# Leaving the 16 meta tokens out of the query side of a hybrid mLSTM / state-space layer

## The reference, cut to what matters

```python
h_p = concatenate([meta_tokens, x_prompt])          # 16 + 256 rows
mix, new = mixer_block(rmsnorm(h), ...)             # scans run over all 272 rows
h = h + mix
if drop_meta: h = h[:, N_META:]                     # the meta rows are dropped here
h = h + hier_moe(rmsnorm(h))
...
s   = (q_t . k_s) * exp(dmat[t, s] - m[t])          # causal, all s <= t
num = s @ v + ...;  den = sum_s s + ...             # mLSTM
h_a = num / max(|den|, exp(-m)) -> rms norm -> * sigmoid(za)
y   = (c_t . b_s) * decay[t, s] * dt[s] @ x + d_skip * x -> * silu(zb) -> group rms norm
out = concatenate([h_a, y]) @ w_out
```

## Time and profile before

| | us |
|---|---|
| median of three runs | 810.22 |
| the runs | 811.71, 810.21, 810.22 |
| span of the profiled execution | 805.8 |
| TensorE / VectorE / ScalarE / GpSimd busy | 772.3 / 291.0 / 217.5 / 29.1 |
| weight loads of TensorE busy | 400.1 |

### The profile page before, as it was taken

The page is one execution under the profiler, slowest core; times in us unless marked ns, Lnnn a source line. Parts: engine busy times, 40 slices in busy tenths (PEclk is TensorE's granted clock), DMA queues, the critical chain, the costliest instruction groups (busy, mean ns, idle before and its releaser), DMA issues.

```text
span 805.8 us, 9663 instructions
## 1 busy us (share of the span) xinstructions
PE 772.3 (96%) x3789; PEld 400.1 (50%) x3789; DVE 291.0 (36%) x722; ACT 217.5 (27%) x612; POOL 29.1 (4%) x85
## 2 busy tenths in 40 slices
PE   7999999998999999999999999999999998999995
PEld 5876777776767778633333333333333333233232
DVE  4945535678988420331130031121120201302204
ACT  4237656728654100340101100101001011001013
POOL 7000000001000100000000000000000000000000
PEclk9999999999999999999999999999999999999998
DMA  9943556675886749479999999999999999999992
GB/s 249 338 165 96 194 168 204 184 260 141 249 276 196 302 155 420 181 283 429 426 427 425 429 428 425 429 425 429 427 427 426 428 425 430 426 428 427 425 403 86
DMA packets 76540, 263.69 MB, mean 327 GB/s; under 512 B 7446, under 2 KB 46618, under 8 KB 62904
## 3 DMA queue, kind: packets, MB, share of 16 engines
q1 hardware_dynamic: 74704, 259.02, 82.3%
q0 software_dynamic: 1568, 3.91, 1.4%
q10 hardware_dynamic: 216, 0.07, 0.1%
HBM read 251.15 MB, written 11.99 MB: 327 GB/s over the span
## 4 chain that ended last, share of the span: by engine, by line
PE 78%; DMA 10%; DVE 7%; ACT 2%; issue 1%; POOL 1%; DVEq 0%; POOLq 0%; ACTq 0%
PE bank L2296 23%; PE bank L2375 11%; PE bank L1869 10%; PE bank L2146 7%; DMA arena<-in_w_down 5%; DMA arena<-in_w_up 5%; PE bank L1857 4%; PE bank L2321 4%; PE bank L2255 3%; PE bank L1962 2%; DVE h_tok L1406 2%; PE bank L2309 1%; PE bank L2265 1%; PE bank L1816 1%; PE bank L2023 1%
## 5 line engine op out<-in xcount | busy, mean ns | idle before, releaser
L2296 PE MATMUL bank<-ring,arena 128*64 128x512 f32 x704 | 159.2, 596 | 5.2 <-DMA ring<-in_w_up 3.7
L1869 PE MATMUL bank<-arena,ring 128*128 128x280 f32 x448 | 113.2, 407 | 3.6 <-DVE arena L1547 1.5
L2296 PEld LDWEIGHTS bank<-ring,arena 128*64 128x64 f32 x704 | 47.9, 137 | 102.2 <-issue 91.0
L1869 PEld LDWEIGHTS bank<-arena,ring 128*128 128x128 f32 x448 | 83.7, 191 | 26.0 <-issue 4.4
L507 DVE COPY arena<-bank 64x512 f32<-64x512 f32 x15 | 10.2, 683 | 205.4 <-PE bank L2375 205.4
L2375 PE MATMUL bank<-ring,arena 128*64 128x512 f32 x304 | 68.1, 593 | 3.0 <-DMA ring<-in_w_down 3.0
L1734 DVE TENSOR_TENSOR arena<-bank,WG 128x512 f32<-128x512 f32 x16 | 16.9, 1057 | 129.8 <-PE bank L2296 129.8
L2146 PE MATMUL bank<-arena,ring 128*128 128x264 f32 x256 | 58.7, 388 | 0.0
L2296 PE MATMUL bank<-arena 128*64 128x512 f32 x240 | 55.6, 598 | 2.0 <-DMA arena<-in_w_up 1.2
L2146 PEld LDWEIGHTS bank<-arena,ring 128*128 128x128 f32 x256 | 48.1, 190 | 9.4 <-issue 1.5
L1200 ACT ACTIVATE arena<-bank 128x512 f32<-128x512 f32 x15 | 9.0, 597 | 147.8 <-PE bank L2309 147.8
(11 more groups left out here) (384 smaller groups left out, 833.9 us busy)
## 6 DMA issues: line engine op xcount, KB each, us to landing
ring<-in_w_gate SPq DMA_DIRECT2D x22, 2048.0 KB, 25.0
ring<-in_w_up SPq DMA_DIRECT2D x22, 2048.0 KB, 28.5
ring<-in_w_down SPq DMA_DIRECT2D x19, 2048.0 KB, 27.2
arena<-in_w_down SPq DMA_DIRECT2D x11, 2048.0 KB, 30.7
ring<-in_w_in SPq DMA_DIRECT2D x9, 2048.0 KB, 11.7
arena<-in_w_up SPq DMA_DIRECT2D x5, 2048.0 KB, 25.3
arena<-in_w_gate SPq DMA_DIRECT2D x5, 2048.0 KB, 30.9
out<-h_tok SPq DMA_DIRECT2D x16, 512.0 KB, 5.2
```

The costliest lines, as they stand in the source:

```text
L1869: last = mm(b[:, 0:T], slot_k(UNIT_SLOT[u], 512)[:, k, o:o + P], hT[:, k, :], start=(k == 0), stop=(k == KD - 1))
L2296: last = mm(b[CAP * half:CAP * (half + 1), :], XG[:, k, (e % 2) * CAP:(e % 2 + 1) * CAP], w(kk)[:, half * 512:(half + 1) * 512], start=(k ...
```

## The change

The query side leaves out the meta columns. Gate tiles, queries, the first of three blocks of scores, weighted sums and denominators, the squares and their sums, the heads' and groups' scales and the gate products run over columns 16 to 280 (or 272, or 304) where they ran from 0. Keys, values, the convolution, `xbc` tiles and states stay as they are, and so do all waits, the order on each engine and all transfers. The core of the diff:

```diff
+Q_FROM = [META, 128, 256]
-BLK = [0, NP, NP + NP - 128]
+BLK = [0, NP - META, NP - META + NP - 128]
...
-            nc.vector.scalar_tensor_tensor(out=YB[:, c, 0:NP], in0=CBX[:, c, 0:NP], scalar=XE[:, c, 16:17],
-                                           in1=bank[6 if c % 2 == 0 else 0][:, 0:NP], op0=ALU.mult, op1=ALU.add)\
+            nc.vector.scalar_tensor_tensor(out=YB[:, c, META:NP], in0=CBX[:, c, META:NP], scalar=XE[:, c, 16:17],
+                                           in1=bank[6 if c % 2 == 0 else 0][:, META:NP], op0=ALU.mult, op1=ALU.add)\
...
-                a.activation(qT[:, h % 2, :], bank[0][:, 0:W], ACT.Copy).then_inc(s.q_sb, 1)
+                a.activation(qT[:, h % 2, META:W], bank[0][:, META:W], ACT.Copy).then_inc(s.q_sb, 1)
...
-                a.activation(dst[:, n % KD, :], z_bank(n)[:, 0:T], ACT.Tanh, scale=0.5).then_inc(signal, 1)
+                a.activation(dst[:, n % KD, META:T], z_bank(n)[:, META:T], ACT.Tanh, scale=0.5).then_inc(signal, 1)
...
-                    w = NP - t0
-                    last = v.scalar_tensor_tensor(out=ARG[0:m, n % 2, BLK[j]:BLK[j] + w], in0=b[0:m, t0:NP],
-                                                  scalar=TM[0:m, j, key:key + 1], in1=mask[0:m, 0:w],
+                    q0 = Q_FROM[j]
+                    last = v.scalar_tensor_tensor(out=ARG[0:m, n % 2, BLK[j]:BLK[j] + NP - q0], in0=b[0:m, q0:NP],
+                                                  scalar=TM[0:m, j, key:key + 1], in1=mask[0:m, q0 - t0:NP - t0],
...
-                link(v.reciprocal(SCL[0:HA, :], SCL[0:HA, :]))
+                link(v.reciprocal(SCL[0:HA, META:T], SCL[0:HA, META:T]))
...
-            def b5_tile(u, o, use, b=bank[5]):
+            def b5_tile(u, o, use, b=bank[5], q0=0):
...
-                    last = mm(b[:, 0:T], slot_k(UNIT_SLOT[u], 512)[:, k, o:o + P], hT[:, k, :], start=(k == 0), stop=(k == KD - 1))
+                    last = mm(b[:, q0:T], slot_k(UNIT_SLOT[u], 512)[:, k, o:o + P], hT[:, k, q0:T], start=(k == 0), stop=(k == KD - 1))
...
-                b5_tile(U_Z + n // 4, (n % 4) * P, B5_Z + earlier, z_bank(n))
+                b5_tile(U_Z + n // 4, (n % 4) * P, B5_Z + earlier, z_bank(n), META)
...
-                mm(bank[0][:, 0:W], wq[:, h, :], XC[:, h, :], start=True, stop=True).then_inc(s.q_ps, 1)
+                mm(bank[0][:, META:W], wq[:, h, :], XC[:, h, META:W], start=True, stop=True).then_inc(s.q_ps, 1)
...
-                mm(bank[7][0:HA, 0:NP], strip[:, 7 - h:15 - h], SQT, start=(h == 0), stop=(h == HA - 1),
+                mm(bank[7][0:HA, META:NP], strip[:, 7 - h:15 - h], SQT, start=(h == 0), stop=(h == HA - 1),
...
-                mm(bank[3][:, 0:T], col(ident[0:HA, :], k), SCL[0:HA, :], start=True, stop=True).then_inc(s.hbc_ps, 1)
+                mm(bank[3][:, META:T], col(ident[0:HA, :], k), SCL[0:HA, META:T], start=True, stop=True).then_inc(s.hbc_ps, 1)
```

More of the change, by code:

```diff
@@ L272, in y_sq @@
         def y_sq(c):
-            return rowt(9 + c % 3, NP)
+            return rowt(9 + c % 3, NP - META)
         h_tok = sb("h_tok", [P, 3, D])
@@ L1505, in denominators @@
             def denominators():
[L1507 to L1511, removed]
+                rows = bank[7][32:32 + HA, META:T]
+                link(v.tensor_copy(DEN[0:HA, META:T], rows))
@@ L1513, in head_squares @@
+                link(v.scalar_tensor_tensor(out=DEN[0:HA, META:T], in0=DEN[0:HA, META:T], scalar=-1.0, in1=DEN[0:HA, META:T], op0=ALU.mult, op1=ALU.max))
+                link(v.tensor_tensor(DEN[0:HA, META:T], DEN[0:HA, META:T], ENM[0:HA, META:T], ALU.max))
+                link(v.reciprocal(DEN[0:HA, META:T], DEN[0:HA, META:T]))
             def head_squares():
                 dve.wait_ge(s.sq_ps, HA + 1)
-                link(v.tensor_tensor(SCL[0:HA, :], bank[7][0:HA, 0:T], DEN[0:HA, :], ALU.mult))
@@ L1587, in _ @@
                     dve.wait_ge(s.gbc_ps, c // 4 + 1)
-                v.scalar_tensor_tensor(out=YB[:, c, :], in0=bank[7 if c < 4 else 3][:, 0:T],
-                                       scalar=PV[:, V_NB + c:V_NB + c + 1], in1=YB[:, c, :],
+                v.scalar_tensor_tensor(out=YB[:, c, META:T], in0=bank[7 if c < 4 else 3][:, META:T],
+                                       scalar=PV[:, V_NB + c:V_NB + c + 1], in1=YB[:, c, META:T],
                                        op0=ALU.mult, op1=ALU.mult).then_inc(s.yb_norm, 1)
@@ L1952, in head_proj, with block_mm @@
                 v_rows(2).then_inc(s.vt_ps, 1)
-            def block_mm(b, c0, lhs, rhs, key, start, accumulate):
+            def block_mm(b, lhs, rhs, start, accumulate):
                 for j, (t0, m) in enumerate(S_TILES):
-                    w = NP - t0
+                    q0 = Q_FROM[j]
                     if accumulate:
-                        o = b[:, c0 + t0:c0 + NP]
+                        o = b[:, q0:NP]
                     else:
-                        o = b[0:m, BLK[j]:BLK[j] + w]
-                    last = mm(o, lhs(j, t0, m), rhs(j, t0, m, w), start=(start and (j == 0 or not accumulate)),
+                        o = b[0:m, BLK[j]:BLK[j] + NP - q0]
+                    last = mm(o, lhs(j, t0, m), rhs(j, q0, m), start=(start and (j == 0 or not accumulate)),
                               stop=(j == 2 or not accumulate))
@@ L2084, in group_sum @@
                 pe.wait_ge(s.sq_done, HA + c + 1)
-                mm(bank[7][64:64 + NG, 0:NP], strip[:, 7 - g_:9 - g_], y_sq(c), start=(c == 0), stop=(c == KD - 1),
+                mm(bank[7][64:64 + NG, META:NP], strip[:, 7 - g_:9 - g_], y_sq(c), start=(c == 0), stop=(c == KD - 1),
                    skip_group_check=True).then_inc(s.sq_ps, 1)
@@ L2137, in _ @@
                         pe.wait_ge(s.st_done, HA + h + 1)
-                        last = mm(yb[q0:q0 + HD, t0:NP], XDT[0:m, j, h * HD:(h + 1) * HD], ARG[0:m, q, BLK[j]:BLK[j] + NP - t0],
+                        tq = Q_FROM[j]
+                        last = mm(yb[q0:q0 + HD, tq:NP], XDT[0:m, j, h * HD:(h + 1) * HD], ARG[0:m, q, BLK[j]:BLK[j] + NP - tq],
                                   start=(j == 0), stop=(j == 2), skip_group_check=True)
@@ L2186, in _ @@
             for j in range(NG):
-                mm(bank[7 if j == 0 else 3][:, 0:T], ident[64:64 + NG, 64 + j:65 + j].to_broadcast([NG, P]), YSC,
+                mm(bank[7 if j == 0 else 3][:, META:T], ident[64:64 + NG, 64 + j:65 + j].to_broadcast([NG, P]), YSC,
                    start=True, stop=True).then_inc(s.gbc_ps, 1)
```

44 lines of the change are left out of this document (23 added, 21 removed).

## The result

The changed kernel takes 805.98 us, the median of five runs (805.33 to 806.36), against 810.22 us before (four runs of 810.20 to 811.71 us; a fifth, of 4,456.88 us, is on record with no explanation, and the median is the same without it). The ratio is 0.9954, with a 95% interval of 0.9940 to 0.9967: faster by 4.2 us, and beyond the 0.2% that a measurement can tell. The forecast was 806.2, with a range of 805.0 to 808.4.

A forecast was written before the change was run, and what follows sets the result against it. Transfers pace the second half, but its expert stream starts when the mixer's chain allows. Gains of 0.71 + 0.03 + 0.49 + 0.55 + 2.07 + 0.19 = 4.04 us took 810.2 to 806.2 us, range 805.0 to 808.4.

The forecast's parts named there:

- What bounds the kernel: Transfers pace the second half, but the expert stream's start hangs on the mixer, so an earlier mixer end moves the end equally.
- rival D: The expert stream's start does not follow the mixer because a transfer holds it; time stays at 810.2 us, chance 0.05.
- Stretch 1: Heads, to 160 us, on TensorE: 26 narrower products gain 0.71 us, upper bound 0.87 if six squares' sums counted too.
- stretch 2: 160 to 172 us, on VectorE: one product and one block, each 16 columns narrower, gain 0.03 us.
- Stretch 3: 172 to 187.5 us, on TensorE: z tiles 0 and 1, a decay product and a squares' sum gain 0.49 us.
- stretch 4: 187.5 to 224.16 us, on VectorE: narrower instructions for three pairs, row products and the reciprocal gain 0.55 us.
- Stretch 5: 224.16 to 268.6 us, on TensorE: eight z tiles (1.75 us) and small products of four pairs (0.33) gain 2.07 us.
- Stretch 6: 268.6 to 290.3 us, on TensorE: four head rows, one squares' sum and two broadcasts gain 0.19 us.
- Stretch 7: From 290.3 us on: gate products are covered by output products and the experts have no such column, so no gain.
- Rival A and B: Clock falls: A, once near 224 us, 807.9 us, chance 0.14; B, repeatedly in 224.2 to 268.6 us, 813.0 us, chance 0.04.
- Rival C: Weight loads or issue pace TensorE's z tiles and small products: 807.9 us at half gain, 809.6 at none, chance 0.10.
- terms 1 and 4: The gains of Stretch 1 (0.71 us, at most 0.87) and stretch 4 (its reciprocal 0.10, at most 0.11).

The follow-up runs named there:

- e2: The changed kernel run again without edits: 806.24 us, ratio 0.9957 to the kernel before.
- e5: The changed kernel with z tiles 8 to 15 narrowed further, to 232 columns, leaving out 32 more tokens: single execution 800.23 us.
- e7: The kernel before with only the squares' sum reading less and the denominator and scale rows 16 columns narrower: single execution 810.03 us beside a median of 809.98.
- e1: The kernel before run again without edits: 809.76 us beside 809.64 for before on the same chip, ratio 1.0006.
- e3: The changed kernel with only z tiles 8 to 15 made as wide as before again (280 columns): 807.22 us, ratio 0.9971 to the kernel before.
- e6: The changed kernel with z tiles 8 to 15 narrowed further, to 136 columns, leaving out 128 more tokens: single execution 797.15 us.
- e12: The changed kernel with three spare matmuls in TensorE's first wait, ahead of the gates' product: 807.17 us, ratio 0.9965 to the kernel before.
- e9: The changed kernel with small products spread between matmuls of the last two 280-column tiles and ScalarE's rows one tile earlier: 812.41 us, ratio 1.0037 to before.

## Why the prediction was right, and where it was not

**What bounds the kernel** held. From the first of the last 168 records of output products to the end are 515.5 us before, 515.8 us in e2 and 515.9 in e5, so the stream followed the mixer, and rival D is out. After's own profile has 516.6 us, 0.8 of them from the clock's fall at 342 us. The first output product came at 266.26 us; with the 1.56 us taken off by which everything started later that is 264.70, the predicted 264.7 (to this digit by luck, see below).

**Stretch 1, heads**, 0.71 us, of which 0.03 lies ahead of head 0's second tile: the piece from there to z tile 0, with stretch 2's 0.03 in it, was predicted at 0.71 and measured 0.70. Counting the squares' sum once was right (e7).

**Stretch 3**, 0.49 us: measured 0.49.

**Stretches 2 and 4**, VectorE: 0.55 us predicted for stretch 4, measured 0.51 between the two first profiles and 0.71 between e1 and e2. Before itself varies by 0.18 us there (its longer one, e1, has the fall of double length at 198 us), so this term is right in size, and no finer. The 0.03 us of stretch 2 can't be parted from stretch 1's. VectorE's products went from 581 to 564 ns, the predicted 17 ns:

```profile
L1442 DVE TENSOR_TENSOR arena<-bank,arena 128x400 f32<-128x400 f32 x24 | 13.5, 564 | 38.4 <-PE bank L1963 35.3 <-ACT arena L964 1.6 <-issue 1.4
...
L1523 DVE RECIPROCAL ring<-ring 8x264 f32<-8x264 f32 x1 | 1.8, 1783 | 0.0
```

**Stretch 5**, 2.07 us: measured 2.03, of which e3 gives back 1.70 with the eight z tiles alone (1.75 by the count).

**Stretch 6**, 0.19 us: measured 0.19. **Stretch 7**, nothing: nothing, beyond the fall of the clock in one profile.

**Rival A and B**: in no profile but e6's does the clock fall between 210 and 330 us. The gap before 218.9 us did get longer, from 0.5 us to 0.6 us in e2 and 1.3 us in after, with the 1.5 us at z tile 8 behind it, and the clock stayed at 1.00. The fall at 197 us, on which rival A was built, isn't shown to come from the wait ahead of it either: after waits 2.6 us there and keeps its clock. In e6, where TensorE's gaps repeat in every pair, the clock did fall at 254 us:

```profile
255.00:256.00 1.00, 1.00 (x5) 0.53 (x6) 0.96 (x4) 0.00 (x0) 0.00 (x0) 0.50 0.00 0
```

That is one fall in one profile, in gaps that the change doesn't have, and the clock also falls with no gap at 53 us; so whether the gaps placed it isn't shown. e6's single execution lay 12.8 us below before's median all the same. **Rival C** is out by e3, e5 and e6, and 3.92 us were measured in the stretches 1 to 6, not half.

**How close the sum came** is partly luck. The pieces from head 0's second tile on give 3.92 us between before and after, for 4.01 predicted, and 4.11 between e1 and e2. The 4.04 comes out only with the 0.12 us of the first piece, which swings by 0.2 us between the pairs, and stretch 4 varies by 0.18 us within before alone. What the traces bear out is every term in its place to within 0.2 us, and not the second digit of the sum. The low end of the range doesn't come out of its own terms: the upper bounds of terms 1 and 4 and half a microsecond, 0.16 + 0.01 + 0.5 us off 806.2, are 805.5 us and not 805.0. The measured 805.98 lies inside either.

**One step was wrong**, though without harm to the result: the base of the sum. I took the 4.4 us between before's span and its median for what lies around the instructions. What lies around them is 1.7 to 1.9 us. The other 2.6 us were the distance from that profiled execution to the median: it had one fall of the clock before 60 us, where e1's had two and a first 280-column product 2.3 us later. Taking 4.0 us off the median was still right in kind, since the shorter pieces came again in each profile. That 806.2 met 805.98 so closely also needed a matching draw: from e1's sample of before (809.64 us beside it) the same 4.0 us would give 805.6 for e2's 806.24. But the check "compare the two spans" that a reader would make first gave 1.4 us, and would have spoken for a result a third as large as it is.

The Trainium skill ("TensorE: Matmul & The Clock Gate", section "Back-to-back issue gap") puts the spacing in a stream of loads and matmuls down to both. Here it was set by the columns, at 264 as at 232, and nearly so at 136 (2.05 against 2.01 us a tile).

## What to carry to other kernels

Cut the chain at marks that both traces have, and compare it piece by piece: the spans of two single executions differed by 1.4 us, while the same pieces gave 4.04 and, in a second pair of profiles, 4.02. A width that shrinks everywhere pays only on the engine that is full in each stretch: six z tiles restored cost nothing, eight restored 40 us later cost 1.70 us. And before small work is moved to make an engine denser, see what it covers and which transfers wait for the work that it now delays: spreading it made the kernel 6.7 us slower.

## What the runs showed that I had not expected

The same program sees its clock fall in different places from one execution to the next. Over the profiles of before and after it fell at 14 to 17, at 19 to 23, at 53 to 58, at 197 to 205 or at 342 to 345 us, in different sets. A fall is some 3.4 us at the 1.2 GHz level (1.7 us of work), or twice that (e1 and e7 at 198 to 205, e12 at 53 to 59), or three times (e9 at 69 to 80). The one at 53 us in before's profile follows no wait of TensorE: it is busy for all of 51 to 57 us, at first on products of 16 and 17 columns. I take the falls for what makes the two groups of before's times, some 2 us apart, but that rests on one profile of each group; the mean granted clock of the executions doesn't part the groups (0.990 to 0.993 in e1's lower one, 0.988 to 0.991 in the upper). A few profiles of the same kernel are needed before a microsecond in a span means anything.
